# The rows of a rank-small product: 48 or 128 rows of TensorE for the keys' decays

## The reference

```python
h = _rms(x, o_norm)
q, k, v, z, f_logit = split(h @ o_w_in)            # 4 x 2048 columns and 16
q, k = _rms(q, q_gain), _rms(k, k_gain)            # head by head
c = cumsum(log_sigmoid(f_logit + b_f))             # 16 heads x 256 positions
s = q k^T * 128**-0.5 + c[query] - c[key]          # causal, softmax
x = x + (softmax(s) v * silu(z)) @ o_w_out
```

## Time and profile before

| | us |
|---|---|
| median of 3 runs (1001.91 to 1003.41) | 1002.88 |
| the profiled execution's own time | 1002.98 |
| its span, first to last instruction | 1001.3 |
| TensorE busy with products | 985.7 (98%) |
| VectorE busy | 630.1 (63%) |
| ScalarE busy | 570.2 (57%) |
| GpSimd busy | 97.9 (10%) |
| mean rate of transfers | 163 GB/s |

### The profile page before, as it was taken

How to read it: one execution, slowest core, us unless ns; L and a number is a source line. 1 busy time by engine, 2 the same in 40 slices (tenths; PEclk the granted TensorE clock), 3 DMA queues, 4 the chain that set the end, 5 groups by cost and what they waited for, 6 DMA issues and landing times.

```text
span 1001.3 us, 14468 instructions
## 1 busy us (share of the span) xinstructions
PE 985.7 (98%) x5315; PEld 833.0 (83%) x5315; DVE 630.1 (63%) x992; ACT 570.2 (57%) x926; POOL 97.9 (10%) x92
## 2 busy tenths in 40 slices
PE   7999999999999999999999999999999999999998
PEld 7988788887887999888888778887888788878887
DVE  4687798898889755665555454545455545555543
ACT  4697657667567655654455554455544654465332
POOL 3101012012021010000002200220022002200000
PEclk9999999999999999999999999999999999999999
DMA  8874434334433447565799965666999856645562
GB/s 275 204 204 152 148 126 130 122 108 127 130 107 122 127 127 263 166 202 189 170 168 176 167 161 168 174 183 135 170 155 175 169 166 180 175 145 166 205 216 84
DMA packets 113859, 163.63 MB, mean 163 GB/s; under 512 B 19222, under 2 KB 54155, under 8 KB 113547
## 3 DMA queue, kind: packets, MB, share of 16 engines
q1 hardware_dynamic: 99504, 159.67, 60.2%
q10 hardware_dynamic: 14298, 3.22, 1.6%
HBM read 160.76 MB, written 2.10 MB: 163 GB/s over the span
## 4 chain that ended last, share of the span: by engine, by line
PE 95%; ACT 4%; DMA 1%; issue 1%; SPq 0%; DVE 0%; ACTq 0%
PE bank L451 23%; PE bank L453 22%; PE bank L452 22%; PE bank L478 4%; PE bank L479 4%; PE bank L480 4%; PE bank L703 1%; PE bank L688 1%; PE bank L593 1%; PE bank L518 1%; ACT wh L939 1%; ACT uz L1051 1%; PE bank L595 1%; PE bank L672 1%; PE bank L584 1%; PE bank L673 1%
## 5 line engine op out<-in xcount | busy, mean ns | idle before, releaser
L947 DVE TENSOR_TENSOR wl<-raw,wh 128x1024 fp32r<-128x1024 f32 x295 | 361.3, 1229 | 282.4 <-ACT wh L939 281.4
L939 ACT ACTIVATE wh<-raw 128x1024 fp32r<-128x1024 f32 x295 | 310.0, 1057 | 170.1 <-PE bank L453 128.3
L451 PE MATMUL bank<-wh,xh 128*128 128x512 f32 x768 | 310.9, 405 | 0.0
L453 PE MATMUL bank<-wh,xl 128*128 128x512 f32 x768 | 300.7, 392 | 0.0
L452 PE MATMUL bank<-wl,xh 128*128 128x512 f32 x768 | 300.1, 391 | 0.0
L453 PEld LDWEIGHTS bank<-wh,xl 128*128 128x128 f32 x768 | 144.3, 188 | 31.7
L451 PEld LDWEIGHTS bank<-wh,xh 128*128 128x128 f32 x768 | 144.4, 188 | 30.2 <-DVE wl L947 0.4
L452 PEld LDWEIGHTS bank<-wl,xh 128*128 128x128 f32 x768 | 144.8, 188 | 26.9
L451 PE MATMUL bank<-wh,yh 128*128 128x512 f32 x256 | 100.8, 394 | 1.4 <-ACT scr L1342 1.4
L453 PE MATMUL bank<-wh,yl 128*128 128x512 f32 x256 | 99.9, 390 | 0.0
L452 PE MATMUL bank<-wl,yh 128*128 128x512 f32 x256 | 99.8, 390 | 0.0
(11 more groups left out here) (323 smaller groups left out, 1120.4 us busy)
## 6 DMA issues: line engine op xcount, KB each, us to landing
raw<-in_o_w_in SPq DMA_DIRECT2D x128, 512.0 KB
raw<-in_e_w_in SPq DMA_DIRECT2D x130, 256.0 KB, 3.3
raw<-in_e_w_out SPq DMA_DIRECT2D x32, 512.0 KB
raw<-in_o_w_out SPq DMA_DIRECT2D x32, 512.0 KB
raw<-in_e_w_in SPq DMA_DIRECT2D x31, 512.0 KB
raw<-in_s_w_glu SPq DMA_DIRECT2D x8, 512.0 KB
res<-in_x SPq DMA_DIRECT2D x8, 256.0 KB, 6.7
res<-in_x SPq DMA_DIRECT2D x1, 2048.0 KB, 8.3
```

The costliest lines, as they stand in the source:

```text
L451: nc.tensor.matmul(o, l_hi, w_hi, start=first, stop=False)
L453: mm = nc.tensor.matmul(o, l_lo, w_hi, start=False, stop=last)
L939: nc.scalar.activation(wh[:, j % RING, :], raw[:, j % RING, :], ACT.Copy).then_inc(hi_done, 1)
L947: nc.vector.tensor_tensor(wl[:, j % RING, :], raw[:, j % RING, :], wh[:, j % RING, :].bitcast(F32), ALU.subtract).then_inc(lo_done, 1)
```

## The change

The product that adds the decays sums over all 128 rows instead of 48. `ones_r`, `nks`, `sel` and `nck` get 128 rows. The clearing of `nks` and the two copies that fill `ones_r` and `sel` cover them all, so `nks` and `sel` are zero in rows 48 to 127 and `nck` is too. The number of instructions, their order, their waits and the columns of each operand stay as they are, and every buffer stays at its offset within a partition.

```diff
-        nks = carve("scr", T, parts=48)
-        sel = carve("scr", 16, parts=48)
+        nks = carve("scr", T)
+        sel = carve("scr", 16)
...
-        nck = wf2[0:48, :, :].rearrange("p a b -> p (a b)").rearrange("p (h t) -> p h t", h=2)
-        ones_r = sb("ones_r", [48, P], F32R)
+        nck = wf2.rearrange("p a b -> p (a b)").rearrange("p (h t) -> p h t", h=2)
+        ones_r = sb("ones_r", [P, P], F32R)
...
                 if s == 14:
                     link(v.memset(nks, 0.0))
-                    v.tensor_copy(ones_r[:, :], ones[0:48, :])
-                    v.tensor_tensor(sel, ident[0:48, 0:16], ident[0:48, 32:48], ALU.add)
+                    v.tensor_copy(ones_r[:, :], ones)
+                    v.tensor_tensor(sel, ident[:, 0:16], ident[:, 32:48], ALU.add)
```

## The result

The changed kernel takes 989.91 us (median of 4 runs, 989.56 to 991.33) against 1002.55 us for the kernel before in the same comparison. The ratio is 0.9871, 95% interval [0.9856, 0.9886], so about 12.9 us less (the two medians alone differ by 12.6). Forecast were 11.7 us less, 991.2 us, with a range of 989.8 to 993.3. By the ratio the changed kernel takes 0.9871 x 1002.55 = 989.6 us, just under that range; its median is at the very edge of it.

The account below looks back on a forecast made before the run. TensorE's own order of work was taken as the bound; four row changes made a head's scores 2.07 us instead of 1.34, so 16 x 0.73 = 11.7 us off 1002.9 gave 991.2 us, range 989.8 to 993.3.

Parts of the forecast that it names:

- What bounds the kernel: Whole kernel: TensorE is 95% of the chain that ended last, so time its own order gives up is saved.
- The leads: Weight splits for the next units: done 5.5 us ahead, so TensorE coming 0.73 us earlier was costed at nothing.
- Four changes for a head: Around line 595: each switch between 128 and 48 rows costs 0.20 us; four give 0.80 less some 0.06.
- loads stay exposed: Rival for the scores block: only the 0.09 us wait per change goes, gain 5.8 us, 997.1 us; chance 0.04.
- 16 heads x 0.73 us = 11.7: Second-layer scores: each head's block falls from 2.07 to 1.34 us, saving 11.7 us over 16 heads.
- 0.5 us on each side: Allowance for the spread of three runs (1.5 us lowest to highest), widening 990.3 to 992.8 into 989.8 to 993.3.
- my sum of 1.34: A head's scores block at 128 rows, L453 to first L451: 0.23 + 0.43 + 0.12 + 0.22 + 0.11 + 0.23 us.
- the sum's own bounds of 10.1 to 12.6: All 16 heads: 10.1 us if five seams keep 0.02 us each, 12.6 if line 595 and L451 take the least.
- VectorE: `fox_keys` (line 1840) stays at 0.34 us, bound 2.2 us in all; clearing and copies at most 1.4 us, all hidden.
- Transfers took nothing back: Rival in the scores stage: the weights' rate is the true bound, TensorE waits out the 11.7 us, 1002.9; chance 0.02.
- The rows are not the cause: Rival at line 595: the gap has another reason, at most 0.3 us changes, 1002.9 to 1003.2 us; chance 0.03.
- slower: Rival at line 451 behind a head's scores: TensorE waits for DVE's slipped split, 1005 us; chance 0.02.

Follow-up runs that it names:

- the order of 48 rows: Against the kernel before: 48 rows kept, line 593 runs for both pieces first, then line 595 for both; 995.99 us, ratio 0.9933.
- the first piece alone: Against the changed kernel: first piece (256 columns) keeps 128 rows, second piece (128 columns) reads only 48; 995.96 us, ratio 0.9931 to the kernel before.
- the step between 64 and 96 rows: Two kernels, the kernel before with the decay product at 64 rows (1002.65 us, ratio 0.9992) or 96 rows (989.82 us, ratio 0.9865).
- The second comparison: The changed kernel once more, unaltered, against nine runs of the kernel before; 990.88 us, ratio 0.9878.
- the change in the first layer: Against the changed kernel: first-layer score products (line 518) go from 64 to 128 rows, queries written twice with zeros; 987.01 us, ratio 0.9845 to the kernel before.

## Why the prediction held in its mechanism and missed in size

**What bounds the kernel.** Right: TensorE's order of work was the bound. Between the first and the last head's scores the changed kernel gains its 11.6 us, and no row of TensorE waiting has come up behind them. The leads were not used up.

**Four changes for a head.** Right, and shown by the order of 48 rows (two changes, half the gain), by the first piece alone, and by the step between 64 and 96 rows. The price is the one of the prediction: 0.09 us without a product and an exposed load of 0.11, in all 0.17 to 0.19 us a change, since a small product hides part of the load. The Trainium skill says in "TensorEngine Tiling (Array Packing)", Key Properties, that changing the tiling mode drains TensorE, and lists in "Available Configurations" arrangements of 128, 64 and 32 rows. The runs agree: the block falls from 2.07 to 1.35 us between 64 and 96 rows, and in the earlier trace rows the step from 32 to 37 rows takes 0.18 us against 0.06. That the array itself is rearranged is the page's account; the runs show when the time is lost, not what happens in it.

**The loads.** The rival "loads stay exposed" would have left a block of 1.7 us; it is 1.35. The load of line 595 starts under line 593's second pass (566.29) though both use all 128 rows. The Trainium skill's rule as the prediction took it ("TensorE: Matmul & The Clock Gate", Part 3, "The mechanism": a load overlaps products in flight only when the row group differs) does not hold in this kernel. The same section also lets a load into the background weight buffer go ahead; whether that happens here no run shows.

**The sum, and the step that failed.** The term "16 heads x 0.73 us = 11.7" was too small; it measured 12.1. The spread between executions was larger than this error, and the range allowed it only "0.5 us on each side". The forecast of 991.2 us lies 1.6 us above the 989.6 that the first comparison's ratio gives. The parts:
- *The block itself*: 0.72 us, not 0.73 (1.35 against my sum of 1.34).
- *Behind the block*: the sum ended at the first L452 and put everything after it at nothing. By the rows of line 595 the gain is (11.6 - 0.27) / 15 = 0.755 us for a head, where 0.27 is what the inside of one block gives between its two products (0.73 before, 0.46 after). So 0.03 us for a head come from the products after it: from that L452 to the next turn (line 584, at 571.64 before and 569.72 after) it is 2.56 us before and 2.53 after. Why they run closer was not isolated. 16 x 0.755 = 12.1 us, 0.4 more than forecast and inside the sum's own bounds of 10.1 to 12.6.
- *The starting point*: I subtracted from 1002.88, the median of three runs; in the comparison the kernel before has 1002.55, 0.3 us less.
- *The spread*: the rest of the first comparison, 0.8 of 12.9 us, is not the change. The second comparison gives 12.2, and 1.1 us of the profiled spans lie in the first layer.

The two comparisons, each with four runs of the changed kernel, differ by 0.97 us in its median, so 0.5 us was too little. The bounds of the sum should have been kept apart from a spread of about 1 us. Which side of 989.8 the first comparison fell on was chance: the second gives 990.9 us, inside the range, with the same kernel.

**VectorE.** Right: line 1840 went from 340 to 347 ns, 16 x 0.007 = 0.1 us on an engine that waits. The clearing of `nks` takes 272 ns as before, the two copies 10 ns more each.

**The other rivals.** Transfers took nothing back: ACT's waits for them are 8.0 us against 7.3 (10.3 in the second profile), and in neither profile does TensorE wait in that stage. "The rows are not the cause" and "slower" fell with the first runs.

## What to carry to other kernels

A product whose operands have 48 or 64 rows between products of 128 costs two changes, 0.17 to 0.19 us each here, beside the time of its own columns; fill its rows with zeros, or put several such products in a row. The sign in a profile is idle time of the weight loads with no semaphore behind it; it names only part of the places, 16 of 32 loads here, so read the distances around such a product too. If the filling needs work on another engine, ask first what TensorE waits for there: in the first layer a quarter of the gain went that way.

## What the runs showed that was not expected

A smaller number of columns in the stationary operand may cost the same. In the changed kernel the first loads of line 672 (fp32, 32 columns) and line 765 (fp32, 64 columns) come late behind a big product, with the releaser "issue":

```profile
134.30 0.14 PEld L672 LDWEIGHTS bank<-res,scr 128*32 128x32 f32 x2 [0.35 <-issue]
73.44 0.25 PEld L765 LDWEIGHTS bank<-con,scr 128*64 128x64 f32 x3 [0.35 <-issue]
```

Both products start 0.32 us behind their L453 (133.98 and 73.12), as line 518 with its 64 rows did before the change in the first layer, where 0.23 is usual. Line 862 (fp32r, also 32 columns) starts 0.22 us behind its L453, no later than any big product:

```profile
524.29 0.39 PE L453 MATMUL bank<-wh,xl 128*128 128x512 f32 x1
524.51 0.28 PE L862 MATMUL bank<-xh,wf 128*32 128x256 f32 x1
```

The format is one difference between them, but not the only one. No run tried to change either, so what decides is open.
